# How decode keys and queries are spread over the partitions in a hybrid S5 / Mamba-2 / retention decoder step: TensorE transposes or DMA from a DRAM scratch

## The chip, the cores and the metric

The kernel runs on one core of one Trainium2 chip. The metric is the device time of one execution in microseconds; before the change it is 1655.92 us (median of 3 runs, 1654.31 to 1656.34).

## What is computed

Two layers of a decoder trunk, for one prompt of 256 tokens and for 8 single-token samples at position 2048 at once. All of it is fp32. Per layer:

```python
proj = rmsnorm(h) @ w_in                       # u, z, xbc, dt, q, k, v, g, gates: 10256 columns
y_a = glu(gelu(s5(u)) @ w_s5_out)              # branch A
y_b = gated_group_rmsnorm(ssd(conv_silu(xbc), dt), z) @ w_ssd_out      # branch B: 16 heads of 64, state 128
y_c = (per_head_norm(retention(rotary(q), rotary(k), v)) * silu(g)) @ w_ret_out   # branch C: 4 heads, v 256, state 128
h += (gate0 * y_a + gate1 * y_b + gate2 * y_c) @ w_out
h += square(relu(rmsnorm(h) @ w_mlp_up)) @ w_mlp_down
```

Branches B and C keep a state S per head. For a sample it is one step of

```python
S = decay * S + outer(v, k)      # per head; retention: 4 x 256 x 128, SSD: 16 x 64 x 128, so 1024 x 128 either way
y = S @ q
```

and the new states are outputs. The states of one sample and branch are 512 KB in and 512 KB out; with 8 samples, 2 branches and 2 layers there are 32 such steps.

## The kernel before

Features lie on the 128 partitions and the 264 tokens (256 of the prompt, 8 samples) on the free axis. One large SBUF tensor, `arena`, holds everything; `small` is a second one. Every projection is a **unit** of 8 blocks of 128 output features; a block is 8 matmuls of 128x264, which the profile lists as 16 records (two for each). A unit's weights come in four DMAs of 1 MB (256 columns each) from SyncE's queue into a ring of four places; a place is refilled when TensorE has used it (L372). In the order of the program a layer has the units u, x0, x1, qk, v, g, z, s5a, s5b, gate0, reto, gate2, gate1, ssdo, wo, then the MLP. All five engine programs are written out by hand, and everything on an engine or a DMA queue goes in program order. PSUM has 8 banks. Banks 0 to 3 take the units' blocks in turn, so block b may start when block b - 4 has been drained (copied out) by ScalarE or VectorE (`bank_free`); where a unit ends, the count runs on into the next. Banks 4 to 7 take the small **fills** in turn (`open_fill`, `FILL`): the order is the list that `mixer_fills` returns, and a fill waits until the one before it in its bank is drained.

**The sample states.** `advance` and `outer_products` do one step n (0 to 7 retention, 8 to 15 SSD), with the state as 8 blocks [128, 128] in one of three places of `dec`. The keys and queries of a sample are columns [128, 1] of `qk` and `xc`, and are needed as rows of 128, the same on every partition. `spread` (L636 to L641) makes them so on TensorE: a transpose of a column broadcast to 128x128, four per fill, one fill for the keys and one for the queries of a sample.

- TensorE: `spread_ret(b)` stands before blocks 0, 1, 3, 5, 7 of s5a and 0, 2, 3 of s5b (`RET_SAMPLE_AT`); `spread_ssd(b)` before the odd blocks of reto and the even blocks of gate2.
- ScalarE, at the same blocks: `outer_products(n)` issues the load of state n + 1 (`load_state`, L1103; it waits until the store of state n - 2 has landed, since that has its place), then makes v * k with 8 copies of 128x128 from the keys' PSUM bank (L902), then issues the store of state n - 1 (`store_state`, L1107). The drain of the unit's block comes after all this.
- VectorE: `advance(n)` does 8 multiply-adds (L1672), then 8 reductions with the queries' PSUM bank (L1678).

After retention sample 7, VectorE copies the 8 results into `v` (L1751, semaphore `ret_yc`). ScalarE waits for that before it drains block 4 of s5b, and TensorE needs that drain for block 0 of gate0. The mean squares of branch C follow (`group_means("rn")`, L747) before block 1 of gate0.

**Branch B of the prompt** lies in unit reto. Per head pair m: TensorE spreads decays (L780), VectorE turns them into log decays (L1806, L1807), ScalarE takes exponentials (L1233), POOL multiplies them with the scores (L1990), and TensorE computes the head outputs (L795, L797). VectorE does `advance(8 + m // 2)` after the odd m. Ahead of reto, fill `sc` (L757, L759) gives columns that ScalarE copies and VectorE uses to weigh the values (L1785, L1786).

Of the kernel before, what the change touches and what calls it, by code (L numbers as in the profile page):

```python
# [12 lines left out]
P = 128  # L13
# [136 lines left out]
def mixer_fills(lyr):  # L150
# [37 lines left out]
PER_LAYER = dict(conv_y=16, conv_t=16, conv_silu=16, gelu_arg=8, gelu_tanh=8, rope_done=8, g_silu=8, z_silu=8, exp_ready=16, exp_masked=16)  # L188
# [14 lines left out]
def build_trunk(nc, t):  # L203

    ctx = ExitStack()
    with ctx:
# [145 lines left out]
        stout = view(O_STOUT, NB, P)  # L352
        zg = view(O_ZG, NB, TOK)
# [9 lines left out]
        with nc.Block() as block:  # L363
# [69 lines left out]
            def _(pe):  # L433
# [81 lines left out]
                def mixer(lyr, with_prep):  # L515
# [120 lines left out]
                    def spread(name, column):  # L636

                        o = open_fill(name)
                        for j in range(4):
                            mm = pe.transpose(o[:, j * P:(j + 1) * P], column(j).to_broadcast([P, P]), ident)  # L640
                        close_fill(mm, name)  # L641

                    def spread_ret(b):
                        spread(f"rkb{b}", lambda j: qk[:, 4 + j, SEQ + b:SEQ + b + 1])
                        spread(f"rqb{b}", lambda j: qk[:, j, SEQ + b:SEQ + b + 1])

                    def spread_ssd(b):
                        spread(f"skb{b}", lambda j: xc[:, 8 + j, SEQ + b:SEQ + b + 1])
                        spread(f"sqb{b}", lambda j: xc[:, 12 + j, SEQ + b:SEQ + b + 1])

                    def s5_states_and_steps():
# [14 lines left out]
                        close_fill(mm, "dt")  # L666

# [66 lines left out]
                    def ret_sample(unit_name):  # L734
                        def at_block(b):
                            if (unit_name, b) in RET_SAMPLE_AT:
                                spread_ret(RET_SAMPLE_AT[unit_name, b])
                        return at_block
# [1288 lines left out]
```

## Time and profile before

| | |
|---|---|
| median of 3 runs | 1655.92 us |
| profiled execution, its own time | 1657.92 us |
| its span | 1656.0 us |
| TensorE matmul busy | 1594.0 us, 96% of the span |
| VectorE / ScalarE / POOL busy | 46% / 26% / 9% |
| granted TensorE clock, mean | 0.99 |
| DMA moved | 239.74 MB, mean 145 GB/s |

The span is what the profiler recorded between the first and the last instruction; the execution's own time is 1.9 us longer, and 2.0 us above the median of the runs. The stretches that matter here come once per layer: the retention samples (325 to 391 us in layer 0, 1130 to 1195 us in layer 1) and reto with gate2 (429 to 517 us and 1234 to 1322 us).

### The profile page before, as it was taken

To read this page: it belongs to the slowest core of one execution; us is meant where nothing else is said; L and a number is where in the kernel's file an instruction comes from. 1 tells how busy PE (TensorE), PEld (TensorE's weight loads), DVE (VectorE), ACT (ScalarE), POOL (GpSimd) and SP (SyncE) were. 2 spreads that over 40 slices of the span, in tenths; PEclk is the share of its full clock that TensorE was granted. 3 is DMA by queue.
4 is the path that set the end of the run, shared out by engine and by line. 5 is a ranking of instruction groups with operands and counts; after the bars stand their busy time and mean duration, and the time that the engine had idled before them with its cause. 6 is when DMAs were issued, how large, how long until landed. Compare 5 with 4: busy or idle time off the path is not lost.

```text
span 1656.0 us, 20670 instructions
## 1 busy us (share of the span) xinstructions
PE 1594.0 (96%) x8006; PEld 1354.8 (82%) x8006; DVE 761.5 (46%) x2248; ACT 424.8 (26%) x1151; POOL 146.7 (9%) x260
## 2 busy tenths in 40 slices
PE   7999799999999999999999999999999999999998
PEld 5888698787778788888888888978787878888887
DVE  3968963455665421551117497516556642111001
ACT  2123143533242222100001332353423322111001
POOL 0004700000120000000000074000003000000000
PEclk9999999999999999999999999999999999999999
DMA  9433414276366347544444343324844844444441
GB/s 273 133 92 124 129 52 127 64 226 203 114 202 205 128 156 176 144 146 134 152 135 146 102 144 115 101 89 137 263 129 141 229 140 142 152 142 150 153 151 53
DMA packets 293684, 239.74 MB, mean 145 GB/s; under 512 B 31870, under 2 KB 292590, under 8 KB 293374
## 3 DMA queue, kind: packets, MB, share of 16 engines
q1 hardware_dynamic: 208816, 197.89, 39.1%
q10 hardware_dynamic: 84772, 40.55, 8.9%
q8 instruction: 63, 1.03, 0.3%
q14 instruction: 33, 0.27, 0.0%
HBM read 217.69 MB, written 20.99 MB: 144 GB/s over the span
## 4 chain that ended last, share of the span: by engine, by line
PE 79%; DVE 13%; DMA 4%; ACT 2%; issue 1%; ACTq 1%; DVEq 0%
PE psum L542 52%; PE psum L860 14%; DMA out_new_ret_s<-arena 3%; DVE arena L1672 2%; PE psum L566 2%; ACT arena L902 2%; PE psum L621 1%; PE psum L640 1%; PE psum L623 1%; PE psum L604 1%; DVE arena L1678 1%; PE psum L606 1%; DVE arena L1519 1%; DVE arena L1597 1%; PE psum L510 1%
## 5 line engine op out<-in xcount | busy, mean ns | idle before, releaser
L542 PE MATMUL psum<-arena 128*128 128x264 f32 x4864 | 1110.9, 388 | 5.0 <-DVE arena L1844 5.0
L542 PEld LDWEIGHTS psum<-arena 128*128 128x128 f32 x4864 | 921.4, 191 | 170.6 <-DVE arena L1844 6.6
L902 ACT ACTIVATE arena<-psum 128x264 f32<-128x264 f32 (+14 forms) x490 | 191.7, 414 | 457.7 <-PE psum L542 290.4
L860 PE MATMUL psum<-arena 128*128 128x264 f32 x1024 | 229.6, 385 | 0.0
L860 PEld LDWEIGHTS psum<-arena 128*128 128x128 f32 x1024 | 193.7, 189 | 34.9
L1672 DVE SCALAR_TENSOR_TENSOR arena<-arena 128x128 f32<-128x128 f32 x256 | 71.6, 352 | 71.2 <-ACT arena L902 71.2
L1892 DVE SCALAR_TENSOR_TENSOR arena<-psum,rstd 128x264 f32<-128x264 f32 x64 | 27.5, 433 | 160.0 <-PE psum L542 159.8
L1905 DVE TENSOR_TENSOR arena<-arena,psum 128x264 f32<-128x264 f32 x16 | 6.9, 431 | 197.4 <-PE psum L860 197.4
L902 ACT ACTIVATE arena<-psum,arena 128x128 f32<-128x128 f32 x256 | 69.6, 387 | 67.7 <-DMA out_new_ret_s<-arena 55.0
L902 ACT ACTIVATE arena<-arena 128x264 f32<-128x264 f32 x32 | 16.5, 517 | 262.6 <-DVE arena L1905 219.8
L1311 ACT ACTIVATE arena<-arena 128x264 f32<-128x264 f32 x64 | 27.1, 425 | 190.4 <-DVE arena L1892 187.0
L905 ACT ACTIVATE arena<-psum 128x264 f32<-128x264 f32 x96 | 37.8, 397 | 125.9 <-PE psum L542 125.8
L1982 POOL TENSOR_TENSOR arena<-arena 128x264 f32<-128x264 f32 x16 | 16.2, 1025 | 457.1 <-ACT arena L1209 372.1
L1678 DVE CUSTOM_DVE_ANT_0 arena<-arena,psum 128x128 f32<-128x128 f32 x256 | 55.9, 285 | 1.1
L1519 DVE RECIPROCAL arena<-arena 128x264 f32<-128x264 f32 x16 | 28.8, 1799 | 51.6 <-ACT arena L999 51.6
L1597 DVE SCALAR_TENSOR_TENSOR arena<-arena 128x288 f32<-128x288 f32 x96 | 50.8, 530 | 3.4
L1962 POOL TENSOR_TENSOR arena<-arena 128x128 f32<-128x128 f32 x64 | 34.0, 531 | 175.6 <-DVE arena L1587 170.8
L1688 DVE SCALAR_TENSOR_TENSOR arena<-arena 128x264 f32<-128x264 f32 x16 | 7.8, 490 | 83.8 <-ACTq L1086 83.8
L640 PE MATMUL psum<-arena 128*128 128x128 f32 x256 | 34.4, 275 | 11.6 <-DVE small L1678 11.6
L1990 POOL TENSOR_TENSOR arena<-arena 128x384 f32<-128x384 f32 x32 | 31.6, 1010 | 142.7 <-ACT arena L1233 142.7
L640 PEld LDWEIGHTS psum<-arena 128*128 128x128 f32 x256 | 28.8, 136 | 16.6 <-DVE small L1678 13.0
L1950 POOL MEMSET arena<- 128x256 f32 x2 | 0.7, 362 | 400.9 <-PE psum L542 400.9
(236 smaller groups left out, 1296.0 us busy)
## 6 DMA issues: line engine op xcount, KB each, us to landing
arena<-in_w_in SPq DMA_DIRECT2D x80, 1024.0 KB, 5.3
arena<-in_w_mlp_up SPq DMA_DIRECT2D x32, 1024.0 KB, 5.4
arena<-in_w_mlp_down SPq DMA_DIRECT2D x32, 1024.0 KB, 5.1
arena<-in_w_s_out SPq DMA_DIRECT2D x16, 1024.0 KB, 5.4
arena<-in_state_ret ACTq DMA_DIRECT2D x16, 512.0 KB, 5.4
out_new_ret_s<-arena ACTq DMA_DIRECT2D x16, 512.0 KB, 7.3
arena<-in_state_ssd ACTq DMA_DIRECT2D x16, 512.0 KB, 4.4
arena<-in_w_ret_out SPq DMA_DIRECT2D x8, 1024.0 KB, 5.2
```

Of the source, the lines that this page charges most:

```text
L542: mm = pe.matmul(banks[b % 4][:, 0:TOK], ring[:, c, k, (b % 2) * P:(b % 2) * P + P], rhs[:, k, :], start=(k == 0), stop=(k == 7))
L566: mm = pe.matmul(o[:, j * 72:(j + 1) * 72], gw[:, ri, m, :], u4[:, m, 8:80], start=True, stop=True)
L640: mm = pe.transpose(o[:, j * P:(j + 1) * P], column(j).to_broadcast([P, P]), ident)
L860: mm = pe.matmul(banks[(2 * j + b) % 4][:, 0:TOK], ring[:, c, k, b * P:(b + 1) * P], hid[:, 8 * c + k, :], start=(c == 0 and k == 0), stop ...
L902: return nc.scalar.activation(out, in_, ACT.Copy, scale=scale)
L905: return nc.scalar.activation(out, in_, ACT.Tanh, scale=scale)
L1519: chain.link(V.reciprocal(dst, src))
L1597: ins = V.scalar_tensor_tensor(y, xc[:, k, tap:tap + CONV_OUT], prm[:, wt:wt + 1], y, ALU.mult, ALU.add)
L1672: chain.step(V.scalar_tensor_tensor(st, st, factor(blk, b), outer[:, b % 2, blk, :], ALU.mult, ALU.add))
L1678: ins = V.tensor_tensor_reduce(outer[:, b % 2, blk, :], dec[:, place, blk, :], bank(f"{pfx}qb{b}")[:, c:c + P], 1.0, 0.0, ALU.mult, ALU.ad ...
L1962: G.tensor_tensor(both.rearrange("p w i m -> p w (i m)"), a8w, now, ALU.mult)\
L1990: G.tensor_tensor(ex[:, hd % 2, :], ex[:, hd % 2, :], sc[:, (hd // 4) % 2, :], ALU.mult)\
```

## The change

Once per layer, VectorE gathers the samples' columns of `qk` and of the second half of `xc` (8 blocks x 8 samples each) into two tiles of 128x64, TensorE transposes each of them, ScalarE copies the result [64, 256] to SBUF and stores it (64 KB) in a DRAM tensor `sample_rows`. From there ScalarE's queue loads, per step, the 8 rows of 128 that belong to it (4 of keys, 4 of queries) to all 128 partitions: 512 KB written to SBUF, read from 4 KB of DRAM. Two such tiles are kept for each branch. The loads for samples 0 and 1 of a branch are issued ahead of it; that for n + 1 follows the store of state n - 1 in `outer_products(n)`. The 256 transposes of `spread` are gone, and with them their 64 fills; each layer has one fill `rows` more. Copies and reductions read SBUF instead of PSUM.

```diff
     return (
-        + ["nss", "nsp", "dt"]
+        + ["nss", "nsp", "dt", "rows"]
...
-        + [f for b in range(8) for f in (f"rkb{b}", f"rqb{b}")] + [f"rn{h}" for h in range(4)]
+        + [f"rn{h}" for h in range(4)]
...
-                                         + ([f"sa{m + 1}"] if m < 7 else [])
-                                         + ([f"skb{m // 2}", f"sqb{m // 2}"] if m % 2 else []))] + ["sy7"]
-        + [f for b in range(4, 8) for f in (f"skb{b}", f"sqb{b}")] + [f"sn{h}" for h in range(4)]
+                                         + ([f"sa{m + 1}"] if m < 7 else []))] + ["sy7"]
+        + [f"sn{h}" for h in range(4)]
...
+        scratch = nc.dram_tensor("sample_rows", (DEPTH, 2, NB, SAMPLES, P), F32).ap()
...
+        rows = view(O_STOUT + 640, 2, P, p1=64)
+        picked = [small[:, 0:64], view(O_PRM + PR_VS, 64)]
+        kq = [view(O_VW, 2, NB, P), view(O_DTS, 2, NB, P)]
...
+                    def sample_rows():
+
+                        pe.wait_ge(s["picked"], PER_LAYER["picked"] * (lyr + 1))
+                        o = open_fill("rows")
+                        pe.transpose(o[0:64, 0:P], picked[0], ident)
+                        close_fill(pe.transpose(o[0:64, P:2 * P], picked[1], ident), "rows")
...
                         close_fill(mm, "dt")
+                        sample_rows()
...
-                    unit("s5a", u, ready="gelu_done", before=ret_sample("s5a"))
-                    unit("s5b", u, before=ret_sample("s5b"))
+                    unit("s5a", u, ready="gelu_done")
+                    unit("s5b", u)
...
-                        if m % 2:
-                            spread_ssd(m // 2)
...
-                    unit("gate2", xn, before=lambda b: spread_ssd(4 + b // 2) if b % 2 == 0 else None)
+                    unit("gate2", xn)
...
+                    def keep_rows():
+                        filled(act, "rows")
+                        is_drained(copy(rows, bank("rows")[0:64, 0:2 * P].rearrange("p (a b) -> p a b", a=2)), "rows")
+                        drained(act, "rows")
+                        act.dma_start(scratch[lyr].rearrange("w k b n -> (k b) w n"), rows)\
+                           .then_inc(s["rows_out"], 16)
+
+                    def load_rows(n):
+
+                        act.dma_start(kq[n // 8][:, n % 2, :, :],
+                                      scratch[lyr, n // 8, :, n % 8, :].unsqueeze(0).to_broadcast([P, NB, P]))\
+                           .then_inc(s[f"kq_in{n % 2}"], 16)
...
                     def store_state(n):
-                        drained(act, f"{'rs'[n // 8]}qb{n % 8}")
+                        advanced(n + 1)
...
                         if n < 15:
                             load_state(n + 1)
-                        filled(act, f"{pfx}kb{b}")
+                        act.wait_ge(s[f"kq_in{n % 2}"], PER_LAYER["kq_in0"] * lyr + 16 * (n // 2 + 1))
                         if n >= 2:
-                            drained(act, f"{'rs'[(n - 2) // 8]}qb{(n - 2) % 8}")
+                            advanced(n - 1)
                         for blk in range(NB):
...
+                            ins = copy(outer[:, b % 2, blk, :], kq[n // 8][:, n % 2, keys + blk // 2, :], vcol(blk, b))
+                        ins.then_inc(s["outer_ready"], 1)
                         if b > 0:
                             store_state(n - 1)
+                            if b < 7:
+                                load_rows(n + 1)
...
                     keep_s5_states()
+                    keep_rows()
...
                     store_s5_states()
+                    act.wait_ge(s["rows_out"], PER_LAYER["rows_out"] * (lyr + 1))
+                    load_rows(0)
+                    load_rows(1)
...
                     filled(act, "sc")
+                    load_rows(8)
+                    load_rows(9)
                     is_drained(copy(cols, bank("sc")[:, 0:232]), "sc")
...
+                    dve.wait_ge(s["rope_done"], PER_LAYER["rope_done"] * (lyr + 1))
+                    dve.wait_ge(s["conv_silu"], PER_LAYER["conv_silu"] * (lyr + 1))
+                    for i, src in enumerate((qk[:, :, SEQ:TOK], xc[:, 8:CB, SEQ:TOK])):
+                        V.tensor_copy(picked[i].rearrange("p (a b) -> p a b", a=NB), src).then_inc(s["picked"], 1)
...
-                                                         bank(f"{pfx}qb{b}")[:, c:c + P], 1.0, 0.0, ALU.mult, ALU.add,
+                                                         kq[n // 8][:, n % 2, queries + blk // 2, :], 1.0, 0.0, ALU.mult, ALU.add,
                                                          ys[:, blk, b:b + 1])
-                        is_drained(ins, f"{pfx}qb{b}")
+                        ins.then_inc(s["advanced"], 1)
```

How ScalarE's instructions stand at two retention samples, before (L1103 loads a state, L1107 stores one):

```order
L1103 DMA arena<-in_state_ret 128x8x128 [waits dec_out1_0]
L902 ACTIVATE arena<-psum,arena 128x128 [waits bank_drained2,bank_filled1]
L902 ACTIVATE arena<-psum,arena 128x128 x7
L1107 DMA out_new_ret_s<-arena 128x8x128 [waits bank_drained0]
L902 ACTIVATE arena<-psum 128x264 [waits proj_filled] x2
```

and in the changed kernel, where the load of a state has line L1094, the store L1115 and the load of rows L1109:

```order
L1094 DMA arena<-in_state_ret 128x8x128 [waits dec_out1_0]
L893 ACTIVATE arena<-arena 128x128 [waits advanced,kq_in1]
L893 ACTIVATE arena<-arena 128x128 x7
L1115 DMA out_new_ret_s<-arena 128x8x128 [waits advanced]
L1109 DMA arena<-sample_rows 128x8x128
L893 ACTIVATE arena<-psum 128x264 [waits proj_filled] x2
```

The first copy and the store behind it now stand behind the landing of the rows (`kq_in1`), and a third DMA per sample follows the store.

TensorE at head pair 2 in unit reto, before (L542 the unit's matmuls, L686/L687 scores, L640 the spreads):

```order
L797 MATMUL psum<-arena 64x128
L686 MATMUL psum<-arena 128x256 [waits bank_drained1]
L687 MATMUL psum<-arena 128x128
L780 MATMUL psum<-arena 128x128 [waits bank_drained2]
L780 MATMUL psum<-arena 128x128 x3
L640 MATMUL psum<-arena 128x128 [waits bank_drained3]
L640 MATMUL psum<-arena 128x128 x3
L640 MATMUL psum<-arena 128x128 [waits bank_drained0]
L640 MATMUL psum<-arena 128x128 x3
L542 MATMUL psum<-arena 128x264 [waits act_drained]
```

and in the changed kernel (L547 the unit, L684/L685 scores, L773 decays):

```order
L790 MATMUL psum<-arena 64x128
L684 MATMUL psum<-arena 128x256 [waits bank_drained0]
L685 MATMUL psum<-arena 128x128
L773 MATMUL psum<-arena 128x128 [waits bank_drained1]
L773 MATMUL psum<-arena 128x128 x3
L547 MATMUL psum<-arena 128x264 [waits act_drained]
```

The two fills of the sample are gone, and the scores' fill no longer shares a bank with the queries of the sample before, but with a decay fill.

## Rows read from the trace of the kernel before

**Rows 1.** The page: busy shares (part 1) and the chain that ended last (part 4).

```profile
PE 1594.0 (96%) x8006; PEld 1354.8 (82%) x8006; DVE 761.5 (46%) x2248; ACT 424.8 (26%) x1151; POOL 146.7 (9%) x260
...
PE 79%; DVE 13%; DMA 4%; ACT 2%; issue 1%; ACTq 1%; DVEq 0%
```

**Rows 2.** The line of the spreads, L640, and who made TensorE wait there.

```profile
L640 PE MATMUL psum<-arena x256: 271/272/323, 325.5 to 1313.8; 128*128 128x128 f32 x128
...
  DVE small L1678: 24.7, 12
```

**Rows 3.** Timeline of TensorE after sample 7: start, duration, line, form, count.

```profile
376.75 23.30 PE L542 MATMUL psum<-arena 128*128 128x264 f32 x96
399.89 1.94 PE L747 MATMUL psum<-arena 128*128 128x264 f32 x8
...
1204.90 1.94 PE L747 MATMUL psum<-arena 128*128 128x264 f32 x8
```

**Rows 4.** Timeline of ScalarE and its queue (ACTq), in brackets idle before and releaser.

```profile
353.68 0.37 ACTq L1103 DMA_DIRECT2D arena<-in_state_ret  x1
...
390.51 0.74 ACT L1209 ACTIVATE arena<-arena 128x264 f32<-128x264 f32 x2 [3.30 <-DVE arena L1751]
391.16 0.37 ACT L905 ACTIVATE arena<-psum 128x264 f32<-128x264 f32 x1
...
1195.05 0.74 ACT L1209 ACTIVATE arena<-arena 128x264 f32<-128x264 f32 x2 [3.30 <-DVE arena L1751]
```

**Rows 5.** Stretches between state loads: busy PE, PEld, DVE, ACT, POOL; PEclk, DMA, GB/s.

```profile
344.00:353.70 9.70, 9.70 (x49) 8.32 (x48) 3.62 (x26) 2.84 (x10) 0.00 (x0) 1.00 0.72 218
353.70:362.00 8.30, 8.30 (x47) 7.19 (x46) 3.46 (x24) 2.84 (x10) 0.00 (x0) 1.00 0.85 253
362.00:370.00 8.00, 8.00 (x41) 6.87 (x40) 3.46 (x24) 2.45 (x9) 0.00 (x0) 1.00 0.89 265
370.00:378.40 8.40, 6.14 (x29) 4.90 (x28) 3.46 (x24) 2.73 (x10) 0.00 (x0) 0.91 0.86 250
378.40:384.00 5.60, 5.60 (x22) 4.63 (x21) 2.86 (x19) 2.45 (x9) 0.00 (x0) 0.83 0.76 200
```

**Rows 6.** The page: ScalarE's DMA queue (part 3), landing times (part 6).

```profile
q10 hardware_dynamic: 84772, 40.55, 8.9%
...
arena<-in_state_ret ACTq DMA_DIRECT2D x16, 512.0 KB, 5.4
out_new_ret_s<-arena ACTq DMA_DIRECT2D x16, 512.0 KB, 7.3
```

**Rows 7.** Timeline of TensorE in reto (450 to 460 us) and gate2 (500 us).

```profile
452.85 0.70 PE L686 MATMUL psum<-arena 128*128 128x256 f32 x2 [1.06 <-DVE small L1678]
...
454.16 1.09 PE L640 MATMUL psum<-arena 128*128 128x128 f32 x8
455.08 3.74 PE L542 MATMUL psum<-arena 128*128 128x264 f32 x16
458.75 0.66 PE L795 MATMUL psum<-arena 128*64 128x256 f32 x4
...
500.00 1.04 PE L640 MATMUL psum<-arena 128*128 128x128 f32 x8
500.87 7.32 PE L542 MATMUL psum<-arena 128*128 128x264 f32 x32
```

**Rows 8.** Timeline of VectorE at step 8 (in reto) and step 12 (in gate2).

```profile
447.28 3.73 DVE L1672 SCALAR_TENSOR_TENSOR arena<-arena 128x128 f32<-128x128 f32 x8
451.04 0.29 DVE L1678 CUSTOM_DVE_ANT_0 arena<-arena,psum 128x128 f32<-128x128 f32 x1
...
484.41 2.19 DVE L1672 SCALAR_TENSOR_TENSOR arena<-arena 128x128 f32<-128x128 f32 x8
```

**Rows 9.** Timeline of POOL in reto.

```profile
447.54 2.00 POOL L1990 TENSOR_TENSOR arena<-arena 128x384 f32<-128x384 f32 x2 [4.61 <-ACT arena L1233]
454.74 1.96 POOL L1990 TENSOR_TENSOR arena<-arena 128x384 f32<-128x384 f32 x2 [5.19 <-ACT arena L1233]
```

More of the change, by code:

```diff
@@ L185 @@
 PR_DTW, PR_C16, PR_COLS, PR_VS = 120, 248, 256, 488
-PER_LAYER = dict(conv_y=16, conv_t=16, conv_silu=16, gelu_arg=8, gelu_tanh=8, rope_done=8, g_silu=8, z_silu=8, exp_ready=16, exp_masked=16)
+PER_LAYER = dict(conv_y=16, conv_t=16, conv_silu=16, gelu_arg=8, gelu_tanh=8, rope_done=8, g_silu=8, z_silu=8, exp_ready=16, exp_masked=16,
+                 outer_ready=16, advanced=16, rows_out=16, picked=2, kq_in0=128, kq_in1=128)
 SEMS = """square_sum vec_in s5_in b_in c_in h0_in convst_in head_in dtw_in raw_ready squares xn_ready prm_ready
@@ L634, in mixer @@
                     unit("g", xn, before=in_g)
[L636 to L649, printed above, removed]
+                    def sample_rows():
[3 more added lines that the diff above has]
+                        close_fill(pe.transpose(o[0:64, P:2 * P], picked[1], ident), "rows")
                     def s5_states_and_steps():
@@ L1103, in load_state, with advanced @@
                         act.dma_start(dec[:, n % 3, :, :], states["rs"[n // 8]][0][n % 8]).then_inc(s[f"dec_in{n % 3}"], 16)
+                    def advanced(n):
+                        act.wait_ge(s["advanced"], PER_LAYER["advanced"] * lyr + n)
+                    def keep_rows():
[4 more added lines that the diff above has]
+                           .then_inc(s["rows_out"], 16)
@@ L1117, in outer_products @@
                         for blk in range(NB):
-                            c = (blk // 2) * P
-                            ins = copy(outer[:, b % 2, blk, :], bank(f"{pfx}kb{b}")[:, c:c + P], vcol(blk, b))
-                        is_drained(ins, f"{pfx}kb{b}")
+                            ins = copy(outer[:, b % 2, blk, :], kq[n // 8][:, n % 2, keys + blk // 2, :], vcol(blk, b))
+                        ins.then_inc(s["outer_ready"], 1)
                         if b > 0:
                             store_state(n - 1)
+                            if b < 7:
+                                load_rows(n + 1)
@@ L1665, in advance @@
                     def advance(n, factor):
-                        pfx, b, place = "rs"[n // 8], n % 8, n % 3
-                        drained(dve, f"{pfx}kb{b}")
+                        b, place, queries = n % 8, n % 3, 0 if n < 8 else 4
+                        dve.wait_ge(s["outer_ready"], PER_LAYER["outer_ready"] * lyr + n + 1)
                         dve.wait_ge(s[f"dec_in{place}"], 16 * (n // 3 + 1))
@@ L1749, in mixer @@
                         advance(b, ret_gamma)
-                    drained(dve, "rqb7")
+                    dve.wait_ge(s["advanced"], PER_LAYER["advanced"] * lyr + 8)
                     V.tensor_copy(v[:, :, SEQ:TOK], ys).then_inc(s["ret_yc"], 1)
@@ L1829, in mixer @@
                                                per_block[:, :, 16:17].to_broadcast([P, NB, SAMPLES]), ALU.mult))
-                    drained(dve, "sqb7")
+                    dve.wait_ge(s["advanced"], PER_LAYER["advanced"] * lyr + 16)
                     chain.wait()
```

9 lines of the change are left out of this document (1 added, 8 removed).

## The prediction

> **What bounds the kernel now.** I read the page first: busy shares, then the chain that ended last. TensorE is busy 96% of the span and holds 79% of the chain [rows 1], so the spreads lie on the engine that sets the time; DMA has 4% of the chain. Next the line of the spreads itself: 256 transposes, and behind them 24.7 us in which TensorE waited for VectorE's reductions [rows 2]. That list counts the matmul and weight-load sides apart, so it is no sum to subtract; I go by the timelines. They show two halves of a layer with different limits. In **the retention half** (units s5a and s5b) the start of gate0 hangs on a chain of state loads and stores on ScalarE's queue. In **the SSD half** (reto and gate2) TensorE follows its own program, with short waits. Everything is done twice, and the two layers read alike.
>
> **SSD half, per layer.** Removed are eight pairs of fills. One pair costs TensorE, from the first spread to the next unit block, 0.92 us in reto and 0.87 us in gate2 [rows 7]. Of the eight, four read 0.92 and four 0.87: 7.2 us in all. Removed too is a wait of 1.06 us for the reductions [rows 7]; it occurs three times, twice ahead of scores and once ahead of a spread: 3.2 us. It goes because those fills took the bank that the queries of the sample before had held; the scores now take one last read by the log decays. What is late next is the head output behind it, which needs POOL's product. That product ended at 454.74 + 1.96 = 456.70 us [rows 9]; TensorE came to it at 458.75 us [rows 7], and without the wait and the spread it would come at 456.8 us. So the product is just in time, and I count the whole 3.2 us. Added are two row loads (samples 8 and 9) between the fill `sc` and its copy on ScalarE. One DMA issue holds the queue 0.37 us [rows 4], so with gaps the two cost 0.8 us, and VectorE, then TensorE, wait for this copy. The half gains 7.2 + 3.2 - 0.8 = 9.6 us.
>
> One thing could eat into that. The reductions now read two operands from SBUF. At step 8 the eight multiply-adds, which always did, took 3.73 us with a POOL pair beside them, against 2.19 us at step 12 [rows 8, 9]; the reduction behind them began 1.5 us after POOL was done (451.04 against 449.54 us), so I take 0 for it. The other end is that each of the three later reductions of reto is also stretched by 3.73 - 2.19 = 1.5 us: 4.6 us a layer. The Trainium skill, GPSIMD Engine Reference, Specifications, says that POOL shares its SBUF interfaces with VectorE and contends with instructions that have two SBUF inputs. The slow multiply-adds agree with it, and by it the reductions are exposed now; whether they collide is a question of time only.
>
> **Retention half, per layer.** Here the spreads are free already, in part: what fixes gate0 is not how far TensorE is. Block 0 of gate0 needs the drain of block 4 of s5b, which ScalarE does at 391.16 us, just behind the result of sample 7 (its next work starts at 390.51 us, released by VectorE's copy) [rows 4]. Counting back from the group means at 399.89 us by one block of 3.58 us (7.32 - 3.74 [rows 3, 7]), gate0 began at 396.3 us, and in layer 1 at 1201.3 us. So in layer 0 TensorE was 5.1 us behind that drain and no more. Without eight spreads (7.0 us) and two waits it would be ahead of it. The half can gain at most 5.1 us if the samples keep their pace, and it loses if they fall back.
>
> Their pace is one state load to the next: 9.7, 8.3, 8.0, 8.4 and 5.6 us for samples 2 to 6 [rows 5]. Each cycle waits until a store has landed. The DMA engines are busy 72 to 89% of a cycle [rows 5] with 512 KB in, 512 KB out and most of the time 1 MB of weights. The change adds 512 KB to each. Its price: ScalarE's queue moved 40.55 MB in 8.9% of the span [rows 6], 147 us, so 1.9 us for 0.52 MB of such packets.
> - Before the chain: the two first row loads stand ahead of ScalarE's exponential that VectorE waits for (0.8 us), and the copy and store of the rows ahead of that add some 0.5 us: +1.3 us.
> - Sample 2: its rows are issued behind the store of state 0 and are waited for ahead of the store of state 1. That store has little beside it, so some of the 1.9 us shows: +0.8 us.
> - The cycles: idle DMA time is 2.7 us in the first (0.28 x 9.7), then 1.25, 0.9, 1.2 and 1.3 us. Rows of 1.9 us fit into the first and overrun the others by 0.65, 1.0, 0.7 and 0.6 us: +3.0 us.
> - Sample 7 must wait for its rows behind the store before it: +1.9 us.
>
> The result of sample 7 comes 7.0 us later, gate0 starts at 391.2 + 7.0 = 398.2 us instead of 396.3, and in layer 1 at 1195.7 + 7.0 = 1202.7 instead of 1201.3. TensorE will have stood still for some us before that. What that costs more is in the same row: the six blocks after its idle time at 376 us took 399.89 - 376.75 = 23.1 us instead of 21.5 [rows 3], and the granted clock in the second stretch of it was 0.83 [rows 5], a mean of full speed (2.4 GHz) and the lower level (1.2 GHz); so 1.7 us. The half loses 1.9 + 1.7 = 3.6 us, in layer 1 3.1 us.
>
> Bounds: at best the rows are wholly covered and only 1.3 us remain. Then gate0 starts 3.8 and 4.3 us earlier than now and nothing is paid for the clock. At worst in this case every one of the six row loads costs its full 1.9 us: 1.3 + 11.4 = 12.7 us instead of 7.0, 5.7 us more a layer.
>
> Other edits together: the gather is two small copies, placed before VectorE waits for POOL's scan, on an engine 46% busy [rows 1]; the two transposes follow the `dt` matmuls, and with ScalarE's copy are in the 1.3 us. One copy tile per sample from SBUF instead of PSUM lies on the chain only at sample 7; I take 0.
>
> **Sum.** 2 x 9.6 - 3.6 - 3.1 = 12.5 us. Against the profiled execution, 1657.9 us, that is 1645.4; it stands 2.0 us above the median of the runs, so 1655.9 - 12.5 = 1643.4 us. I round to 1644.
>
> **The rivals.**
> - **The rows are hidden** (0.18). For it: each cycle has an idle tail of about 1 us or more, the time between the end of the data and the next load's first packet, and the rows are queued to run just there. Then 2 x 9.6 + 3.8 + 4.3 = 27.3 us are gained: 1629.
> - **The broadcast reads are slow, and the samples' chain becomes the bound** (0.25): slower than before. No DMA of this trace reads the same bytes many times. Here all 16 DMA engines read the same 4 KB of DRAM, 128 times over, and each load stands ahead of a store that the next load of a state waits for. Each microsecond over 1.9 is paid six times a layer, since the DMA engines have no idle time left in these cycles. The gain of 12.5 us is gone at 1.0 us more per load (12.5 / 12), at 2.9 us. At half the rate, 3.8 us a load, it is 12 x 1.9 = 22.8 us: 1643.4 + 22.8 = 1666. If a load of rows takes the 5.4 us of a state load [rows 6] all by itself, 12 x 3.5 = 42 us: 1685. The Trainium skill, DMA: Bandwidth & Descriptors, Latency and other measured facts, has the nearest rule: copies whose partitions lie a large power of two apart in HBM ran at 103 GB/s instead of 207, and it infers that lock-stepped streams met in one channel. If a stride of zero counts as such, the first of these two times follows; no run so far shows it.
> - **No change** (0.09): the chain loses the full 5.7 us more a layer and some of the collisions with POOL occur: 1643.4 + 11.4 + up to 9 = 1655 to 1664.
> - The forecast itself has 0.48.
>
> **The numbers.** This kernel's runs tell 0.2%, 3.3 us, from no change: 1652.6 to 1659.2. The forecast with its bounds lies from 1636 (half way to the hidden case) to 1655, and nearly all of it is faster; with the hidden case, and the mild end of the others, faster has 0.64. Same takes most of the third rival and the weakest part of the second: 0.11. Slower has 0.25. The range goes from 1630 (the hidden case nearly whole) to 1672 (the second rival at a little over half rate); some 0.1 lies above it and less than 0.1 below.
>
> **What would show each step.** In the changed kernel's profile TensorE's timeline should have no 1.06 us wait ahead of the scores in reto, and a head pair there about 2 us shorter. The loads of rows should land within about 3 us after the store issued just ahead of them; idle time before the first copy of a sample should be put down to `sample_rows`, short. DMA share between 344 and 390 us should be over 0.95. The group means of branch C should come 1 to 4 us later than 399.89 us in layer 0. TensorE should wait on ScalarE's drains in s5b. If the group means come at 396 us, the rows were hidden; if they come after 406 us, or rows take over 3 us by themselves in a quiet stretch, the second rival holds and the total is slower. If reto's pairs are not shorter, the product of POOL or the reductions took the place of the wait.

## The result and the profile after

| | before | changed |
|---|---|---|
| median of the runs, us | 1655.92 (3 runs) | 1751.2 (3 runs, 1750.34 to 1753.63) |
| ratio to before, 95% interval | 1 | 1.058 (1.0559 to 1.060) |
| span of the profiled execution, us | 1656.0 | 1748.4 |

The kernel is 5.8% slower, 95 us. The forecast was 1644 with a range of 1630 to 1672: wrong in sign, and the time lies far above the range. The page of the changed kernel, for the busy shares and the chain [rows 1], ScalarE's DMA queue and its landings [rows 6]:

```profile
PE 1601.3 (92%) x7754; PEld 1348.2 (77%) x7754; DVE 765.3 (44%) x2252; ACT 431.1 (25%) x1153; POOL 145.3 (8%) x260
...
q10 hardware_dynamic: 118340, 57.46, 13.8%
...
PE 66%; DMA 18%; DVE 10%; ACT 3%; ACTq 2%; issue 1%; DVEq 0%
...
arena<-sample_rows ACTq DMA_DIRECT2D x32, 512.0 KB, 11.7
arena<-in_state_ret ACTq DMA_DIRECT2D x16, 512.0 KB, 8.1
out_new_ret_s<-arena ACTq DMA_DIRECT2D x16, 512.0 KB, 5.9
```

TensorE has 252 fewer matrix instructions and yet is busy 7 us more: its mean granted clock is 0.967 instead of 0.990, and the matmuls of the units (x4864) have a mean of 394 ns instead of 388. Of the chain it holds 66% instead of 79, and DMA 18% instead of 4. The rows of a sample take 11.7 us in the median from issue to landing. The next view shows them where little else moves. Timeline of ScalarE and its queue at the first two row loads of layer 0:

```profile
326.51 1.08 ACTq L1109 DMA_DIRECT2D arena<-sample_rows  x2
...
331.18 3.86 ACTq L1094 DMA_DIRECT2D arena<-in_state_ret  x1
335.13 0.40 ACT L893 ACTIVATE arena<-arena 128x128 f32<-128x128 f32 x1 [6.02 <-DMA arena<-sample_rows]
335.34 5.88 ACTq L1094 DMA_DIRECT2D arena<-in_state_ret  x1
...
341.27 2.45 ACT L893 ACTIVATE arena<-arena 128x128 f32<-128x128 f32 x8 [3.42 <-DMA arena<-sample_rows]
```

The first sample's copies start 8.6 us after the issue of their rows, the second's after 14.3 us. These two times are not the load's alone: the issue of a state load stands ahead of each copy on ScalarE, took 3.86 and 5.88 us here instead of 0.37 before [rows 4], and ended within 0.1 us of the copy's start. The windows beside them (the last three numbers are the granted clock, the DMA share and GB/s), and two between state loads, which answer to [rows 5]:

```profile
328.00:330.00 2.00, 2.00 (x11) 1.69 (x10) 1.78 (x2) 1.11 (x3) 0.00 (x0) 1.00 0.29 86
...
365.70:379.00 13.30, 10.37 (x43) 8.32 (x42) 3.73 (x28) 2.99 (x10) 0.00 (x0) 0.93 0.97 205
...
391.20:403.90 12.70, 6.13 (x19) 4.58 (x19) 3.61 (x26) 2.99 (x10) 0.00 (x0) 0.77 0.94 210
```

At 328 us there is room: with both row loads in flight the DMA engines count as busy for 29% of the time only, and deliver 86 GB/s; SyncE issues no weights between 318 and 334 us. So the loads are slow with hardly a rival for the engines, and the busy share doesn't show it. The cycles between state loads, from 354.6 us on, now take 11.2, 13.2, 12.2 and 12.7 us where they took 9.7, 8.3, 8.0 and 8.4 [rows 5]. The rows stand ahead of each store on one queue, and the next state waits for that store, so their slowness is added in every cycle. TensorE pays in the stretch of s5a, s5b and gate0, up to the group means:

```profile
348.63 7.42 PE L547 MATMUL psum<-arena 128*128 128x264 f32 x32 [3.59 <-ACT arena L893]
362.96 9.61 PE L547 MATMUL psum<-arena 128*128 128x264 f32 x32 [6.91 <-ACT arena L893]
375.50 7.42 PE L547 MATMUL psum<-arena 128*128 128x264 f32 x32 [2.93 <-ACT arena L893]
388.09 5.43 PE L547 MATMUL psum<-arena 128*128 128x264 f32 x16 [5.17 <-ACT arena L893]
400.08 9.80 PE L547 MATMUL psum<-arena 128*128 128x264 f32 x32 [6.57 <-ACT arena L896]
411.77 3.81 PE L547 MATMUL psum<-arena 128*128 128x264 f32 x16 [1.89 <-ACT arena L896]
424.26 9.68 PE L547 MATMUL psum<-arena 128*128 128x264 f32 x32 [8.68 <-ACT arena L896]
433.78 1.94 PE L740 MATMUL psum<-arena 128*128 128x264 f32 x8
```

These seven waits sum to 35.7 us, and the group means come at 433.78 instead of 399.89 us [rows 3], 33.9 us late. TensorE is not waiting for rows itself: it waits for drains that ScalarE does in program order behind copies that wait for rows.

The four group means of a run (branch C, then branch D, in both layers) cut the whole loss into stages. Starts, us:

| | C, layer 0 | D, layer 0 | C, layer 1 | D, layer 1 | span |
|---|---|---|---|---|---|
| before | 399.89 | 533.93 | 1204.90 | 1338.94 | 1656.0 |
| changed | 433.78 | 581.12 | 1284.15 | 1431.04 | 1748.4 |
| more than before, by stage | +33.9 | +13.3 | +32.1 | +12.9 | +0.3 |

Some 70% of the loss (66 of 92 us) arise in the retention halves. But 26 us come from the SSD halves, where the forecast had a gain of 9.6 us a layer, which its second rival kept.

### The profile page after: what moved, and what is told of

The parts are those of the page before. It is cut to its first block, busy times and chain, and to the rows that moved or that the text cites. A ratio compares the mean times of both kernels' runs of the same rounds, so it can differ in the third digit from the quotient of the medians.

```text
span 1748.4 us, 20178 instructions
## 1 busy us (share of the span) xinstructions
PE 1601.3 (92%) x7754; PEld 1348.2 (77%) x7754; DVE 765.3 (44%) x2252; ACT 431.1 (25%) x1153; POOL 145.3 (8%) x260
## 3 DMA queue, kind: packets, MB, share of 16 engines
q10 hardware_dynamic: 118340, 57.46, 13.8%
## 4 chain that ended last, share of the span: by engine, by line
PE 66%; DMA 18%; DVE 10%; ACT 3%; ACTq 2%; issue 1%; DVEq 0%
PE psum L547 42%; DMA arena<-sample_rows 18%; PE psum L851 13%; ACT arena L893 3%; PE psum L571 2%; PE psum L626 1%; PE psum L628 1%; PE psum L609 1%; PE psum L611 1%; DVE arena L1534 1%; DVE arena L1612 1%; PE psum L515 1%; PE psum L625 1%; DVE arena L1563 1%; PE psum L662 1%
## 5 line engine op out<-in xcount | busy, mean ns | idle before, releaser
L547 PE MATMUL psum<-arena 128*128 128x264 f32 x4864 | 1138.0, 394 | 98.4 <-ACT arena L896 59.7
L547 PEld LDWEIGHTS psum<-arena 128*128 128x128 f32 x4864 | 938.1, 194 | 280.9 <-issue 47.9
L851 PE MATMUL psum<-arena 128*128 128x264 f32 x1024 | 229.6, 385 | 0.0
L851 PEld LDWEIGHTS psum<-arena 128*128 128x128 f32 x1024 | 193.7, 189 | 34.9
L893 ACT ACTIVATE arena<-arena 128x128 f32<-128x128 f32 (+1 forms) x288 | 94.8, 403 | 482.3 <-DVE arena L1922 219.8
L1326 ACT ACTIVATE arena<-arena 128x264 f32<-128x264 f32 x64 | 27.1, 425 | 190.8 <-DVE arena L1909 186.3
L1999 POOL TENSOR_TENSOR arena<-arena 128x264 f32<-128x264 f32 x16 | 14.6, 930 | 561.2 <-ACT arena L1222 442.0
L1695 DVE CUSTOM_DVE_ANT_0 arena<-arena 128x128 f32<-128x128 f32 x256 | 57.0, 289 | 1.1
L609 PE MATMUL psum<-arena 128*32 128x128 f32 x128 | 25.7, 284 | 10.2 <-DVE arena L1646 10.2
L571 PEld LDWEIGHTS psum<-arena 128*128 128x128 f32 x256 | 29.8, 191 | 0.5
L896 ACT ACTIVATE arena<-arena 128x288 f32<-128x288 f32 (+1 forms) x48 | 19.1, 441 | 42.3 <-DVE arena L1612 39.5
## 6 DMA issues: line engine op xcount, KB each, us to landing
arena<-sample_rows ACTq DMA_DIRECT2D x32, 512.0 KB, 11.7
```

The source lines that it names most:

```text
L547: mm = pe.matmul(banks[b % 4][:, 0:TOK], ring[:, c, k, (b % 2) * P:(b % 2) * P + P], rhs[:, k, :], start=(k == 0), stop=(k == 7))
L571: mm = pe.matmul(o[:, j * 72:(j + 1) * 72], gw[:, ri, m, :], u4[:, m, 8:80], start=True, stop=True)
L609: pe.matmul(o[0:32, j * P:(j + 1) * P], bblk[:, 0, lm, :], eb[:, 0, lm, 0:4, :].rearrange("p a b -> p (a b)"), start=True, stop=False)
L851: mm = pe.matmul(banks[(2 * j + b) % 4][:, 0:TOK], ring[:, c, k, b * P:(b + 1) * P], hid[:, 8 * c + k, :], start=(c == 0 and k == 0), stop ...
L893: return nc.scalar.activation(out, in_, ACT.Copy, scale=scale)
L896: return nc.scalar.activation(out, in_, ACT.Tanh, scale=scale)
```

## Experiments

Three readings were open. **S**: a read of the same few KB by all DMA engines is slow. **Q**: the volume, or the place in the queue, of 512 KB more per sample is what costs. **P**: small packets, read over and over, are what is slow. None of the three names the answer that came out, the distance of the rows; it was found by the probes.

### Isolated transfers: probe

```
for rep in range(2):                         # SyncE, behind the last store; each waits for the one before
  L447 tile <- 1024 distinct rows of 512 B            L452 tile <- 2 sets of 8 rows side by side, 64 partitions each
  L448 wide <- 128 distinct pieces of 4 KB            L453 tile <- 4 sets
  L449 tile <- 8 rows 4 KB apart, for all (as changed) L454 tile <- 16 sets, 4 KB apart
  L450 tile <- 8 rows side by side, for all           L455 tile <- 16 sets, 32 KB apart
  L451 wide <- one piece of 4 KB, for all
```

> The kernel before, with 18 DMAs of 512 KB added behind its last one, each issued from SyncE when the one before has landed, nothing else running: two rounds of nine source patterns into the same 128 partitions. In order: distinct rows of 512 B; distinct rows of 4 KB; one set of 8 rows of 512 B at a pitch of 4 KB for all partitions (as the changed kernel does); 8 rows of 512 B side by side for all; one row of 4 KB for all; then 2, 4 and 16 sets of rows for 64, 32 and 8 partitions each, the 16 once at a pitch of 4 KB and once of 32 KB. Theory S (reads of the same few KB of DRAM by all engines are slow by themselves): distinct rows land in about 4 us, the three patterns with one set in 8 us or more, and the time falls as sets are added, near 4 us at 16. Theory Q (the rows are slow only for what is queued around them): all nine land in about 4 us. Theory P (it is the small packets read over and over): one row of 4 KB for all is near 4 us while 8 rows of 512 B for all are 8 us.

Timeline of SyncE's queue, first round: start of each issue, which is when the one before has landed, so a difference of two starts is the time of one transfer, latency included:

```profile
1653.22 0.39 SPq L447 DMA_DIRECT2D arena<-in_state_ret  x1
1657.00 0.35 SPq L448 DMA_DIRECT2D arena<-in_state_ret  x1
1660.12 0.37 SPq L449 DMA_DIRECT2D arena<-in_state_ret  x1
1668.66 0.33 SPq L450 DMA_DIRECT2D arena<-in_state_ret  x1
1672.22 0.33 SPq L451 DMA_DIRECT2D arena<-in_state_ret  x1
1675.94 0.67 SPq L452 DMA_DIRECT2D arena<-in_state_ret  x1
1688.22 0.56 SPq L453 DMA_DIRECT2D arena<-in_state_ret  x1
1696.77 0.59 SPq L454 DMA_DIRECT2D arena<-in_state_ret  x1
```

All move 512 KB. Distinct rows of 512 B take 3.8 us, the change's form (L449) 8.5 us, but the same sharing of one 4 KB piece (L451) 3.7 us. So a stride of zero over the partitions is not slow in itself, and S as stated is wrong. P expected 8 us for the eight rows side by side (L450), and they took 3.6; but they moved in 144 packets, as the one piece of 4 KB did, and not in the 1040 of L449, so this doesn't decide on P. Two and four sets were no cure, 12.3 and 8.5 us; sixteen took 4.6 (the last section comes back to them). The second round agrees within 0.4 us.

### Volume and place alone: e1_distinct

The row loads stay where they are, with their size and waits, but read a tile of the decode states in place of the scratch. This leaves out the right keys and queries; no time depends on their values.

```diff
-  scratch[lyr, n // 8, :, n % 8, :].unsqueeze(0).to_broadcast([P, NB, P]))\
+  states["rs"[n // 8]][0][n % 8])\
```

> The changed kernel, but a load of rows reads 512 KB of distinct DRAM rows (the state of the same sample and branch) instead of the 4 KB of rows for all partitions; number, size, place in the queue and waits of the DMAs are the same. The samples' results are computed from the wrong keys and queries. Theory S: landings of this load fall from 11.7 us to some 6 us, and the time to near the forecast of 1644 us, 1640 to 1660. Theory Q: it stays at 1750, within 5 us.

Measured: 1651.8 us (10 runs, 1647.1 to 1658.3), ratio to before 0.9976 (0.9959 to 0.9992). Q is refuted: with the same volume at the same place the loss is gone. The landing of these loads has a median of 8.0 us, not the 6 expected.

### One piece of 4 KB per sample: e2_row4k

```diff
-  scratch = nc.dram_tensor("sample_rows", (DEPTH, 2, NB, SAMPLES, P), F32).ap()
+  scratch = nc.dram_tensor("sample_rows", (DEPTH, 2, SAMPLES, NB, P), F32).ap()
-  scratch[lyr].rearrange("w k b n -> (k b) w n")       # store
+  scratch[lyr].rearrange("w b k n -> (b k) w n")
-  scratch[lyr, n // 8, :, n % 8, :]                    # load
+  scratch[lyr, n // 8, n % 8]
-  V.tensor_copy(picked[i].rearrange("p (a b) -> p a b", a=NB), src)
+  V.tensor_copy(picked[i].rearrange("p (b a) -> p a b", a=NB), src)
```

> The changed kernel with the scratch laid out so that the 8 rows of a sample lie side by side, one run of 4 KB per partition instead of 8 of 512 B; all partitions still read the same 4 KB. Theory S: no better than 1730, the bytes are as hot as before. Theory P: an eighth of the packets, landings near 5 us and the time near 1650.

Measured: 1649.1 us (one run). All else of the change is there; the loss is not. The landing is 7.9 us in the median, where 5 were expected. Still two things differ from the change: the distance of the rows, and packets of 4 KB instead of 512 B.

### Distance or packet size: probe2, probe3, e5_pitch

Probe2 again puts single transfers behind the kernel before. In the order of its lines: L453 rows 4 KB apart; L454 side by side, with a gapped destination so that they move as 512 B; L455 1 KB apart; L456 1.5 KB; L457 4.5 KB; L458 8 KB; L459 1024 distinct rows 4 KB apart; L460 one single row, eight times; L461 and L462 as L453, but to 16 and to 64 partitions.

> The kernel before with 20 more transfers on SyncE's queue behind its last store, each alone, ten kinds in two rounds. Nine of them fill 128 partitions x 8 x 128 floats (512 KB) or a part of it. In the first probe eight rows of 512 B at a distance of 4 KB, the same for all partitions, took 8.5 us, and 3.7 us where they lay side by side. Theory A (the distance of 4 KB is what is slow: the rows fall on one place of the memory): 4 KB apart 8.5 us, 8 KB apart 8.5 us or more, 1 KB, 1.5 KB and 4.5 KB apart 3.5 to 5 us, side by side with a gapped destination 3.7 us, one single row for all eight 8.5 us or more, distinct rows at 4 KB 8 us too. Theory B (packets of 512 B out of rows that every engine reads are slow, whatever the distance): all the shared kinds with packets of 512 B 8 to 9 us, side by side with a gapped destination too, and distinct rows at 4 KB 3.8 us. Size: for 16 and 64 of the partitions the same rows take 2 + 6.5/8 = 2.8 us and 2 + 6.5/2 = 5.3 us if the time goes by the packets, and as much as for 128 if it does not.

SyncE's queue in probe2, first round:

```profile
1652.79 0.39 SPq L453 DMA_DIRECT2D arena<-in_state_ret  x1
1661.22 0.39 SPq L454 DMA_DIRECT2D arena<-in_state_ret  x1
1664.80 0.37 SPq L455 DMA_DIRECT2D arena<-in_state_ret  x1
1668.35 0.37 SPq L456 DMA_DIRECT2D arena<-in_state_ret  x1
1671.99 0.37 SPq L457 DMA_DIRECT2D arena<-in_state_ret  x1
1675.56 0.37 SPq L458 DMA_DIRECT2D arena<-in_state_ret  x1
1689.37 0.67 SPq L459 DMA_DIRECT2D arena<-in_state_ret  x1
1693.31 0.38 SPq L460 DMA_DIRECT2D arena<-in_state_ret  x1
1707.88 0.34 SPq L461 DMA_DIRECT2D arena<-in_state_ret  x1
1710.46 0.63 SPq L462 DMA_DIRECT2D arena<-in_state_ret  x1
```

4 KB apart 8.4 us, but 3.6 us at 1, 1.5 and 4.5 KB and side by side, all in packets of 512 B: the distance it is. At 8 KB it takes 13.8 us, nearly as much as one row read eight times over (14.6). Distinct rows 4 KB apart take 3.9 us, against theory A's 8: both are needed, few addresses and the bad distance. Probe3 asks for the rule with ten more kinds, in the order of its lines (L457 on): 2, 4, 8, 16, 3, 6, 5 and 12 KB apart, then pairs of neighbouring rows 4 and 8 KB apart.

> Ten more kinds of isolated transfer behind the kernel before, two rounds, each 512 KB to all 128 partitions out of the same eight rows of 512 B; only the distance of the rows changes. So far: side by side, 1, 1.5 and 4.5 KB 3.6 us, 4 KB 8.3 us, 8 KB and one single row read eight times over 13.7 to 14.6 us. Theory A1 (rows whose addresses agree modulo 8 KB get in each other's way, about 11.7 us divided by the number of different remainders, over 2 us of latency and not under 3.6 us): 2 KB 4.9 us, 4 KB 8.3, 8 KB 13.7, 16 KB 13.7, 3 KB 3.6, 6 KB 4.9, 5 KB 3.6, 12 KB 8.3. Theory A2 (only an equal low part counts, 4 KB being one special step): 2, 3, 5 and 6 KB 3.6 us, 4, 12 and 16 KB alike at 8.3 us. Two rows side by side, then a step of 4 or 8 KB: 4.9 and 8.3 us by A1 if each 512 B is a place of its own, 8.3 and 13.7 us if both rows share one.

SyncE's queue in probe3, the first seven starts behind L457:

```profile
1653.79 0.39 SPq L457 DMA_DIRECT2D arena<-in_state_ret  x1
1658.59 0.38 SPq L458 DMA_DIRECT2D arena<-in_state_ret  x1
1666.90 0.37 SPq L459 DMA_DIRECT2D arena<-in_state_ret  x1
1680.65 0.37 SPq L460 DMA_DIRECT2D arena<-in_state_ret  x1
1694.88 0.37 SPq L461 DMA_DIRECT2D arena<-in_state_ret  x1
1698.54 0.37 SPq L462 DMA_DIRECT2D arena<-in_state_ret  x1
1703.58 0.37 SPq L463 DMA_DIRECT2D arena<-in_state_ret  x1
1707.20 0.37 SPq L464 DMA_DIRECT2D arena<-in_state_ret  x1
```

| distance, KB | 2 | 4 | 8 | 16 | 3 | 6 | 5 | 12 | pairs, 4 | pairs, 8 |
|---|---|---|---|---|---|---|---|---|---|---|
| places by A1 | 4 | 2 | 1 | 1 | 8 | 4 | 8 | 2 | 4 | 2 |
| expected, us | 4.9 | 8.3 | 13.7 | 13.7 | 3.6 | 4.9 | 3.6 | 8.3 | 4.9 | 8.3 |
| first round | 4.80 | 8.31 | 13.75 | 14.23 | 3.66 | 5.04 | 3.62 | 8.15 | 4.83 | 7.77 |
| second round | 4.99 | 8.63 | 15.07 | 13.90 | 3.92 | 4.79 | 3.58 | 7.51 | 4.94 | |

A1 names each within 10%: what counts is how many different remainders modulo 8 KB the eight rows have; A2 is refuted. That is a rule for the distances tried, 0.5 to 16 KB, from one starting address. (The last transfer has no issue behind it, so the second round has no tenth time.) What in the memory stands behind a remainder is an inference, not shown. The Trainium skill, DMA: Bandwidth & Descriptors, Latency and other measured facts, reports slow copies at row distances of 2 to 8 MB, some KB of padding as the cure, and infers that lock-stepped streams meet in one channel. The runs here agree with padding as the cure, at distances a thousand times smaller and for shared rows alone.

The same step inside the kernel, with packets of 512 B kept:

```diff
-  scratch = nc.dram_tensor("sample_rows", (DEPTH, 2, NB, SAMPLES, P), F32).ap()
+  scratch = nc.dram_tensor("sample_rows", (DEPTH, 2, NB, SAMPLES, P + 32), F32).ap()[:, :, :, :, 0:P]
```

> The changed kernel with rows of the scratch padded from 512 to 640 B: the eight rows of a sample lie 5 KB apart and not 4 KB, and still move as packets of 512 B. Theory A (the distance of 4 KB): a row load lands in 8 us in the median, the kernel takes 1650 to 1660 us. Theory B (packets of 512 B that every engine reads): a landing of 11 to 12 us and 1745 to 1755 us, as the change.

Measured: 1651.7 us (one run). One number of the layout, 128 B of padding a row, takes 99.5 us off the changed kernel. Landing times of the row loads in the changed kernel and in e5_pitch (their line's view):

```profile
DMA to landing us min/median/max: 8.0/11.7/16.1
```

```profile
DMA to landing us min/median/max: 4.3/8.0/10.4
```

### Making it worse: e6_pitch8k, e7_pitch2k

```diff
-  (DEPTH, 2, NB, SAMPLES, P)                                e6: rows 8 KB apart
+  (DEPTH, 2, NB, SAMPLES, 2 * P)        ...[:, :, :, :, 0:P]
-  (DEPTH, 2, SAMPLES, NB, P)                                e7, from e2: 2 KB apart
+  (DEPTH, 2, SAMPLES, NB, 4 * P)        ...[:, :, :, :, 0:P]
```

> The changed kernel with rows of the scratch padded to 1 KB, so that the eight rows of a sample lie 8 KB apart: by itself such a load takes 13.7 us, 5.4 us more than in the change. If the row loads are what the samples wait for, the loss grows with it: from the two points so far (3.6 us by itself 1651.7 us, 8.3 us by itself 1751.2 us, so 21 us for each us) the kernel takes 1866 us; at most all 32 loads count, 1924 us. If the change's time hung on something else than the speed of this load (its issue, the queue, the clock), it stays near 1751 us.

> The scratch laid out by sample with rows padded to 2 KB: eight rows 2 KB apart. By theory A1 a load by itself takes 4.9 us and the kernel 1651 us plus at most 21 us for each us over 3.6, so 1651 to 1679 us; by A2 1649 to 1653 us.

| distance of a sample's rows | 5 KB (e5) | 2 KB (e7) | 4 KB (change) | 8 KB (e6) |
|---|---|---|---|---|
| one load by itself, us | 3.6 | 4.9 | 8.4 | 14.1 |
| landing in the kernel, median, us | 8.0 | 9.1 | 11.7 | 18.6 |
| kernel, us | 1651.7 | 1680.9 | 1751.2 | 1917.8 |
| kernel, more per us more by itself | | 23 | 20 | 30 |

(The loads by themselves are means of all the times of that kind, and the last row goes by their unrounded values. e5, e6 and e7 are one run each; the steps between them are 29 us and more.) The kernel follows the isolated time over the whole scale, so the loss comes from how long this load takes. It grows as if some 20 of the 32 loads of a run were paid in full at first, and from 4 to 8 KB nearly all. Both expectations were a little low: e7 lies above its bound of 1679, and e6 took 1917.8 us and not 1866, close to the 1924 at which all 32 loads count.

### What is left of the forecast: e2b_row4k_timed, e4_hybrid, e4b_hybrid

e2b is e2 again, with 4 runs. The hybrid takes from the scratch only the SSD samples; the retention samples keep their spreads and their banks.

```diff
+  # retention: rkb/rqb fills, spread_ret in s5a and s5b, and their waits, as in the kernel before
-  act.wait_ge(s["rows_out"], ...); load_rows(0); load_rows(1)      # behind the S5 states
+  act.wait_ge(s["rows_out"], ...)                                  # ahead of load_rows(8)
-  if b < 7: load_rows(n + 1)
+  if 8 < n < 15: load_rows(n + 1)
```

> The changed kernel with the scratch laid out by sample, so that the eight rows of a sample are one piece of 4 KB; one look at it gave 1649.1 us. If a row load of the ordinary price is all that was missing from the forecast, the median is 1645 to 1652 us and the ratio to the kernel before 0.993 to 0.998. If that look was a lucky one it is 1655 or more.

> As e2b_row4k_timed, but the eight samples of the retention half get their keys and queries by TensorE transposes as before, and only those of the SSD half from the scratch. If the forecast's two halves are right (the SSD half gains 9.6 us a layer, the retention half loses 3.6 us because its samples are then bound by the state's cycle), the group means of layer 0 come at 400 us again and not at 403.6, and the kernel is 2 x 3.6 us faster than e2b: 1638 to 1645 us. If the retention half's loss is made up later in any case (the spreads of TensorE cost as much as they save), it is as fast as e2b, 1646 to 1652 us.

> e4_hybrid again, in more rounds: it gave 1644.3 us (1638.0 to 1647.2) and a ratio to the kernel before of 0.9907. If the row loads are worth having only in the SSD half, the median is 1641 to 1646 us and the ratio's interval lies below that of the kernel with all samples' rows loaded (0.9934 to 0.9964); if the low run was an exception, it is 1645 to 1649 us.

| | median, us | ratio to before, 95% | C, layer 0 | C to D | C, layer 1 | C to D |
|---|---|---|---|---|---|---|
| before | 1656.8 | 1 | 399.89 | 134.0 | 1204.90 | 134.0 |
| e2b | 1649.1 | 0.9949 (0.9934 to 0.9964) | 403.52 | 126.0 | 1204.82 | 125.9 |
| e4 | 1644.3 | 0.9907 (0.9881 to 0.9933) | 401.32 | 126.1 | 1200.35 | 126.3 |
| e4b | 1640.1 | 0.9894 (0.9878 to 0.9911) | 397.40 | 125.9 | 1196.90 | 125.8 |

With a good layout the change is worth 0.5%, and with the retention samples left to TensorE 1.0%: the best version, ahead of both kernels. e4 and e4b are one kernel, and its group means moved by 3.9 us from one profile to the other, so single profiles of that half are to be read with that much doubt. The intervals of e4b and e2b don't meet; e4b's median, 1640.1 us, lies just below the 1641 to 1646 that was expected. From the D means of layer 0 to the C means of layer 1 the hybrid takes 672.9 and 673.6 us, still 2 to 3 us more than the kernel before (671.0); why stays open.

TensorE in e2b around the SSD half, which answers to [rows 7]: two head pairs, one of them with a sample, are now 456.50 - 445.85 = 10.65 us from block to block (12.8 before), and no wait stands ahead of the scores (L684):

```profile
445.85 3.74 PE L547 MATMUL psum<-arena 128*128 128x264 f32 x16
...
455.30 0.70 PE L684 MATMUL psum<-arena 128*128 128x256 f32 x2
...
456.50 3.74 PE L547 MATMUL psum<-arena 128*128 128x264 f32 x16
```

And the last head pair, from the timeline of all engines: POOL's product ends at 480.00 + 1.96 us, and TensorE, there at 480.8, waits for it twice.

```profile
480.00 1.96 POOL L2007 TENSOR_TENSOR arena<-arena 128x384 f32<-128x384 f32 x2 [5.23 <-ACT arena L1248]
...
481.15 0.62 PE L788 MATMUL psum<-arena 128*64 128x256 f32 x2 [0.34 <-POOL arena L2007]
```

## Why the prediction was wrong

**The step that failed** is the price of a row load. "1.9 us for 0.52 MB of such packets" was taken from transfers of other bytes at other distances. The load of this change takes 8.4 us by itself. With another distance of the rows it takes 3.6. The forecast had named the possibility as its second rival, with 0.25, but tied it to the wrong property: not to the sharing alone (3.7 us when all engines read the same 4 KB in one piece), but to shared rows that lie 4 KB apart. The distance could be seen before, in the shape of the scratch, SAMPLES x P x 4 B = 4096 B; that it is a bad one, no trace had shown. And the rival's own times, 1666 and 1685, stopped at 5.4 us a load. The range's end, 1672, is 4.3 us a load by the rival's rule, (1672 - 1643.4) / 12 + 1.9, so a little under half rate and not over it.

**The rival's multiplier was too small as well.** "Paid six times a layer" gives 12 x (8.4 - 1.9) = 78 us and 1721, and even that sum sets a whole duration against a time of occupancy: the 1.9 us are what the packets occupy, and such a load takes 3.6 us by itself. Like with like, the change's load is 4.8 us too long, and twelve of them are 58 us. That is what the retention halves show: against e5_pitch that of layer 0 is 31.2 us longer, and from D of layer 0 to C of layer 1 it is 27.2 us, 58.4 together, so this part of the rival holds. But the SSD half of layer 0 takes 147.34 us instead of 126.77, 20.6 longer, and that of layer 1 is 18.0 longer, where the rival counted no loss. There too ScalarE stood for rows, up to 10.7 us at a time, and the drains behind them came late. TensorE in gate2 of the changed kernel:

```profile
545.62 10.41 PE L547 MATMUL psum<-arena 128*128 128x264 f32 x32 [6.31 <-ACT arena L896]
...
568.63 12.64 PE L547 MATMUL psum<-arena 128*128 128x264 f32 x48 [4.28 <-ACT arena L896]
```

**The other steps held in the main, as the versions with a good layout show.**
- Retention half, a forecast loss of 3.6 and 3.1 us: in e2b the group means came 3.6 us later in layer 0 (403.52), and from the D means to the C means of the next layer it took 4.3 us more (675.3 instead of 671.0). That this half is bound by the samples' cycle and not by TensorE is borne out by the hybrid too, which is faster for giving TensorE the spreads back.
- The price of 1.9 us, as the time that packets occupy the engines, is right for packets of 512 B: in e5_pitch ScalarE's queue holds 12.6% of 1649.7 us, 208 us, 61 more than before for 32 loads, 1.9 us each. In the changed kernel it is 13.8% of 1748.4, 94 more, 2.9 us each, for loads that take 8.4. The share of a queue counts packets and not what lies between them.
- SSD half, a forecast gain of 9.6 us: 8.0 us in e2b. Even in the changed kernel the wait ahead of the scores is gone, and the head pair with a sample is 2.2 us shorter (481.25 to 486.93 us, before 447.24 to 455.08). The two row issues cost 0.8 us as forecast (from the C means to the first decays 35.6 instead of 34.8 us). What is missing is behind that: 8.9 instead of 10.4 us. The product of POOL that was called "just in time" is the cause, with one difference: not in each pair, but in the last, where TensorE takes 5.84 us (476.96 to 482.80) for block and head output, against 4.49 (479.40 to 483.89) before; 1.35 us of the missing 1.5.
- The reductions with two SBUF operands, taken at 0: their line has a mean of 289 ns in the changed kernel, 285 before. That 0 is luck of timing and no sign that POOL and VectorE don't contend there: in the changed kernel, e2b and e5 no reduction ran beside a product of POOL. In e6_pitch8k, with other times, some did, and took up to 1.14 us instead of 0.29, so the forecast's other end was a real danger:

```profile
546.17 2.01 POOL L2007 TENSOR_TENSOR arena<-arena 128x384 f32<-128x384 f32 x2 [4.69 <-ACT arena L1248]
...
547.26 1.07 DVE L1695 CUSTOM_DVE_ANT_0 arena<-arena 128x128 f32<-128x128 f32 x1
```

**The markers.** "If the group means come after 406 us ... the second rival holds" decided rightly (433.8). "Over 3 us by themselves" was set too low: an isolated load takes 3.6 us even when nothing is wrong with it. "Within about 3 us" for the rows to land was far off (11.7 in the median), and the waits put down to them were not short, up to 11.1 us. And the DMA share "over 0.95" between state loads was seen in one window (0.97) of the four (0.75, 0.97, 0.84, 0.94), which says nothing for the forecast: in the busy windows a full queue and a slow one look alike.

## What to carry to other kernels

When the reads of one DMA repeat, write down the addresses that all its streams visit and look at their distance: eight shared rows of 512 B took 3.6 us at 5 KB and 8.4 us at 4 KB by themselves, and a pad of 128 B a row, or one piece per sample, was worth 100 us. A price taken from packets of another pattern is only a lower end; where such a load enters a chain that waits in order, the range must reach to several times that price, times every load of the run, not only those of the half that is bound today. Compare it with a load of the same kind in the same measure: the time by itself and the time that its packets occupy are two numbers (3.6 and 1.9 us here). And a helper that frees TensorE is worth it only where TensorE sets the pace: the same edit gained 8 us a layer in one half and lost 3.6 to 4.3 in the other.

## What the runs showed of the hardware

- Eight rows shared by all partitions are slowed where their addresses agree modulo 8 KB (distances of 0.5 to 16 KB): 8 places 3.6 us, 4 places 4.9, 2 places 8.3, 1 place 14, for 512 KB. A single row of 512 B read 1024 times takes about as long, 14.6 us.
- Distinct rows of 512 B, though all 4 KB apart, took 3.9 us: the distance alone does no harm.
- The time goes with the number of packets: with rows 4 KB apart 2.6 us for 16 partitions, 4.9 for 64 and 8.4 for 128.
- Several copies of the eight rows, each for a part of the partitions, are slower than one even with the rows side by side, where the copies are the outer dimension: one set 3.6 us, 2 sets 12.3, 4 sets 8.5, 16 sets 4.6. The Trainium skill, DMA: Bandwidth & Descriptors, Rules for kernel authors, says that an outer dimension under 16 confines a transfer to that many engines; the two slow cases agree with it, and so do their packets under 512 B, 2 and 4 of them where the transfers with one set or sixteen have 16. Why sixteen sets still take 1 us more than one is not shown.
- The DMA share of a window can be low with a load in flight that others wait for: 0.29 with two row loads in the changed kernel, 0.30 with one alone (probe, 1661 to 1667 us, rows 4 KB apart), 0.15 with rows 8 KB apart (probe2, 1676 to 1688 us).
- While slow row loads are in flight, the issue of the next DMA on the same queue can take long itself: up to 5.88 us for a state load in the changed kernel and 10.15 us in e6_pitch8k, 0.60 us at most before.
- A reduction of 128x128 with both operands in SBUF takes 0.29 us, and 1.07 to 1.14 us beside a product of POOL (e6_pitch8k); eight multiply-adds took 3.73 us beside one and 2.19 without [rows 8, 9].
